# A sixteen-slot ring of expert weights in place of twelve, three of its slots filled during the output projection

## The reference

```python
mixed = concat([o_a, o_b, o_c]) @ w_out                      # (640, 2048) @ (2048, 2048)
x = x + g1 * rms_norm(mixed, g_post_mix)
h = rms_norm(x, g_pre_ffn) * (1 + sc2) + sh2
aff = softmax(h @ w_router)                                  # 16 experts
g, idx = top_k(aff.T, cap)                                   # 64 sample rows, 16 prompt rows each
hid = silu(xs @ w_gate) * (xs @ w_up)                        # per expert 2048 x 1024, twice
y = (hid @ w_down) * g                                       # per expert 1024 x 2048
x = x + g2 * rms_norm(scatter_add(y), g_post_ffn)
```

## Time and profile before

| | us |
|---|---|
| median of three runs | 2994.15 |
| lowest and highest | 2991.12, 3000.06 |
| span of the profiled execution | 2995.6 |
| PE busy in it | 2680.6 (89%) |
| DVE busy | 1331.9 (44%) |
| ACT, POOL busy | 525.4, 482.1 |
| output projection on PE, about | 1567 to 1877 |
| experts on PE, about | 1877 to 2950 |

### The profile page before, as it was taken

How to read it: one execution, slowest core, us unless ns; L and a number is a source line. 1 busy time by engine, 2 the same in 40 slices (tenths; PEclk the granted TensorE clock), 3 DMA queues, 4 the chain that set the end, 5 groups by cost and what they waited for, 6 DMA issues and landing times. The chain is left out here.

```text
span 2995.6 us, 60885 instructions
## 1 busy us (share of the span) xinstructions
PE 2680.6 (89%) x25988; PEld 1534.8 (51%) x25988; DVE 1331.9 (44%) x2353; ACT 525.4 (18%) x1471; POOL 482.1 (16%) x647
## 2 busy tenths in 40 slices
PE   5699999999959599999769999999999999999993
PEld 1366666666637489899634444333333332333330
DVE  1667667767546465666241114422233332222323
ACT  2100000000025355555331111100000000000001
POOL 0100000000065466665140000000000000000000
PEclk8899999999979799999879999999999999999996
DMA  9576555454366312221197888799999999999997
GB/s 409 210 227 208 189 180 197 174 207 173 138 204 129 131 45 53 61 52 40 26 366 267 307 308 324 309 402 404 404 405 404 404 394 396 404 404 403 403 413 290
DMA packets 268517, 783.60 MB, mean 262 GB/s; under 512 B 99473, under 2 KB 163112, under 8 KB 199712
## 3 DMA queue, kind: packets, MB, share of 16 engines
q1 hardware_dynamic: 257104, 724.13, 64.0%
q0 software_dynamic: 10848, 56.51, 6.4%
q10 hardware_dynamic: 368, 0.10, 0.0%
HBM read 712.59 MB, written 68.08 MB: 261 GB/s over the span
## 5 line engine op out<-in xcount | busy, mean ns | idle before, releaser
L2243 PE MATMUL oe_ps<-experts_ring,tail_arena 128*32 128x512 f32 x4096 | 502.8, 605 | 42.6 <-DMA experts_ring<-in_w_up 42.6
L478 DVE SCALAR_TENSOR_TENSOR pj_macc<-pj_mring,head_cond_t,pj_macc 128x1024 f32<-128x1024 f32 x240 | 297.1, 1279 | 182.1 <-DMA pj_mring<-in_w_ada 182.1
L2243 PEld LDWEIGHTS oe_ps<-experts_ring,tail_arena 128*32 128x32 f32 x4096 | 154.5, 111 | 338.8 <-issue 337.8
L551 PE MATMUL pj_ps<-head_hT,head_ring_in 128*128 128x320 f32 x1104 | 312.3, 436 | 6.5 <-DVE head_hT L451 4.2
L2276 PE MATMUL oe_ps<-experts_ring,oe_hidt 128*32 128x512 f32 x2880 | 312.1, 592 | 0.0
L2251 PE MATMUL oe_ps<-experts_ring,tail_arena 128*32 128x512 f32 x2048 | 274.3, 600 | 0.0
L551 PEld LDWEIGHTS pj_ps<-head_hT,head_ring_in 128*128 128x128 f32 x1104 | 210.9, 191 | 96.6 <-DVE head_hT L451 6.5
L2580 DVE SCALAR_TENSOR_TENSOR oe_hid_s<-oe_hid_s,oe_gcol_s,oe_ps 128x512 f32<-128x512 f32 x16 | 12.0, 748 | 535.6 <-ACT oe_hid_s L2426 535.6
L2322 PE MATMUL oe_ps<-experts_ring,tail_arena 128*128 128x512 f32 x520 | 232.5, 604 | 15.5 <-DMA tail_arena<-scratch_o 15.5
L551 PE MATMUL pj_ps<-pj_t,pj_s 128*128 128x320 f32 x736 | 210.4, 440 | 6.8 <-DVE pj_t L457 6.8
L2276 PEld LDWEIGHTS oe_ps<-experts_ring,oe_hidt 128*32 128x32 f32 x2880 | 110.2, 110 | 198.8 <-issue 198.8
(11 more groups left out here) (423 smaller groups left out, 3893.0 us busy)
## 6 DMA issues: line engine op xcount, KB each, us to landing
experts_ring<-in_w_gate SPq DMA_DIRECT2D x128, 1024.0 KB, 24.6
experts_ring<-in_w_up SPq DMA_DIRECT2D x128, 1024.0 KB, 26.2
experts_ring<-in_w_down SPq DMA_DIRECT2D x128, 1024.0 KB, 21.7
experts_ring<-in_w_out SPq DMA_DIRECT2D x68, 1024.0 KB, 6.9
pj_mring<-in_w_ada SPq DMA_DIRECT2D x64, 1024.0 KB, 9.5
head_ring_in<-in_w_in SPq DMA_DIRECT2D x23, 2048.0 KB, 7.9
ada_ring<-in_w_ada SPq DMA_DIRECT2D x16, 2048.0 KB, 19.8
scratch_z<-pj_stage POOLq DMA_DIRECT2D x19, 640.0 KB, 8.1
```

The lines of the kernel that those rows point to most:

```text
L478: a = nc.vector.scalar_tensor_tensor(acc, w, scalar, acc, ALU.mult, ALU.add)
L551: mm = pe.matmul(bank(name, b)[:, 0:TH], a[:, k, :], h[:, k, :], start=(k == 0), stop=(k == KH - 1))
L2243: pe.matmul(ps[32 * i:32 * i + 32, bank, :], xe[:, k, GROUPS[i % 2]], w[:, kk * DE + 512 * (i // 2):kk * DE + 512 * (i // 2) + 512], start ...
```

## The change

The ring gets sixteen slots: the twelve places of `experts_ring` and places 0, 1, 2 and 9 of the arena. Slab `n` goes to slot `n % 16`. Slabs 0 to 2, whose places (9 to 11) are not used by the projection, are loaded behind three chosen slabs of `w_out` in its third and fourth tile; slabs 12 to 15 are loaded when the last tile's `h2` and routing are done. Since 24 slabs an expert are not a multiple of sixteen, the loops of SP and PE now take two experts a pass. `EARLY` is half of the number of slots, so it goes from 6 to 8. What `block_final` reads changes places: `x1` and the gains go to ring slots 0 to 6, each when its slab of the last down but one is used.

```diff
+MORE = (0, 1, 2, 9)
+NSLOT = len(SLOTS) + len(MORE)
+
+FINAL_X, FINAL_G, FINAL_F = (0, 1, 2, 3, 4), (5, 6), (7, 8, 9, 10, 11)
+FINAL_FG, FINAL_JUNK = (0, 1, 2, 9, 5), 7
...
+def slot_of(ring, arena, n):
+
+    i = n % NSLOT
+    return ring[:, SLOTS[i], :] if i < len(SLOTS) else arena[:, MORE[i - len(SLOTS)], :]
...
-    SLOTS_IN = len(slot_in)
+    SLOTS_IN = NSLOT
+    FREE_AT = [(2, 3), (2, 9), (3, 3)]
...
+                if (t, j) in FREE_AT:
+                    load(0, FREE_AT.index((t, j)), FREE_AT.index((t, j)))
-            for n in range(SLOTS_IN):
-                if n >= 6:
+            for n in range(len(FREE_AT), GU):
+                if n >= len(SLOTS):
+                    if n == len(SLOTS):
+                        sp.wait_ge(h2r, NT)
+                        sp.wait_ge(routed, NT)
+                elif n >= 6:
                     sp.wait_ge(w_used, NT * SLABS - 11 + n)
-                elif n >= 3:
+                else:
                     sp.wait_ge(w_used, LAST * SLABS + 1)
-                load_expert(sp, weights, w_all, slot_in, 0, n, n)
-            for n in range(SLOTS_IN, GU):
-                load_expert(sp, weights, w_all, slot_in, 0, n, n, used=(slot_used, n - SLOTS_IN + 1))
-            with sp.Fori(1, NE) as e:
+                load(0, n, n)
+
+            def expert_loads(e, n, it):
+
                 for i in range(GU):
...
+                    load(e, i, n + i, used=(slot_used, n + i - SLOTS_IN + 1 + it * PER))
...
+            with sp.Fori(1, NE - 1, 2) as e:
+                expert_loads(e, GU, e - 1)
+                expert_loads(e + 1, GU + PER, e - 1)
+            expert_loads(NE - 1, GU + (NE - 2) * PER, 0)
...
             for t in range(NT):
-                sp.dma_start(arena[:, FINAL_X[t], :], x1_d[t]).then_inc(x1_in[t], 16)
+                sp.wait_ge(slot_used, base - DN + FINAL_X[t] + 1)
+                sp.dma_start(w_all[:, SLOTS[FINAL_X[t]], :], x1_d[t]).then_inc(x1_in[t], 16)
...
-            with pe.Fori(2, NE - 1) as e:
-                expert(e)
+            expert(1, GU, None)
+            with pe.Fori(2, NE - 2, 2) as e:
+                expert(e, GU + PER, e - 2)
+                expert(e + 1, GU + 2 * PER, e - 2)
+            expert(NE - 2, GU + (NE - 3) * PER, None)
```

More of the change, by code:

```diff
@@ L1991, in _, with load_expert @@
                 finish_pair(q)
-def load_expert(sp, weights, ring, slot_in, e, r, n, used=None):
+def slot_of(ring, arena, n):
+    i = n % NSLOT
+    return ring[:, SLOTS[i], :] if i < len(SLOTS) else arena[:, MORE[i - len(SLOTS)], :]
+def load_expert(sp, weights, ring, arena, slot_in, e, r, n, used=None):
     w_gate, w_up, w_down = weights
-    slot = n % len(slot_in)
-    place = SLOTS[slot]
+    slot, place = n % NSLOT, slot_of(ring, arena, n)
     e = bass.ds(e, 1)
@@ L2003, in load_expert @@
         src = w[0, e, (r // 2) * 256:(r // 2 + 1) * 256, :].rearrange("o (p k) f -> p (o k) f", p=P)
-        dst = ring[:, place, :].rearrange("p (k f) -> p k f", k=2)
+        dst = place.rearrange("p (k f) -> p k f", k=2)
     else:
         src = w_down[0, e, (r - 16) * P:(r - 15) * P, :].rearrange("o p f -> p (o f)")
-        dst = ring[:, place, :]
+        dst = place
     if used:
@@ L2116, in _, with load @@
                 sp.dma_start(crow[(2 + cnd) * KD:(3 + cnd) * KD, :], mod_d[cnd, 3 * D:4 * D].rearrange("(k p) -> k p", p=P)).then_inc(once, 16)
+            def load(e, r, n, used=None):
+                load_expert(sp, weights, w_all, arena, slot_in, e, r, n, used)
             for n in range(RING, NT * SLABS):
@@ L2136, in _ @@
                 for i in range(DN):
-                    load_expert(sp, weights, w_all, slot_in, e - 1, GU + i, 2 * GU + i, used=(slot_used, (e - 1) * PER + 2 * GU + i - SLOTS_IN + 1))
+                    load(e - 1, GU + i, n + i, used=(slot_used, n + i - SLOTS_IN + 1 + it * PER))
+            with sp.Fori(1, NE - 1, 2) as e:
+                expert_loads(e, GU, e - 1)
+                expert_loads(e + 1, GU + PER, e - 1)
+            expert_loads(NE - 1, GU + (NE - 2) * PER, 0)
             base = GU + (NE - 1) * PER
@@ L2139, in _ @@
             for i in range(DN):
-                load_expert(sp, weights, w_all, slot_in, NE - 1, GU + i, base + i, used=(slot_used, base + i - SLOTS_IN + 1))
+                load(NE - 1, GU + i, base + i, used=(slot_used, base + i - SLOTS_IN + 1))
             for t in range(NT):
-                sp.dma_start(arena[:, FINAL_X[t], :], x1_d[t]).then_inc(x1_in[t], 16)
+                sp.wait_ge(slot_used, base - DN + FINAL_X[t] + 1)
+                sp.dma_start(w_all[:, SLOTS[FINAL_X[t]], :], x1_d[t]).then_inc(x1_in[t], 16)
@@ L2143, in _ @@
             for cnd in range(2):
-                sp.dma_start(arena[:, FINAL_G[cnd], :], bcast_rows(cst_d, (3 * cnd + 2) * D, D)).then_inc(g2_in, 16)
+                sp.wait_ge(slot_used, base - DN + FINAL_G[cnd] + 1)
+                sp.dma_start(w_all[:, SLOTS[FINAL_G[cnd]], :], bcast_rows(cst_d, (3 * cnd + 2) * D, D)).then_inc(g2_in, 16)
         @block.gpsimd
@@ L2235, in slabs_of @@
             def slabs_of(j, n0):
-                return w_all[:, SLOTS[(n0 + 2 * j) % SLOTS_IN]], w_all[:, SLOTS[(n0 + 2 * j + 1) % SLOTS_IN]]
+                return slot_of(w_all, arena, n0 + 2 * j), slot_of(w_all, arena, n0 + 2 * j + 1)
             def sample_step(xe, j, kk, n0):
@@ L2630, in sem @@
             return nc.alloc_semaphore("fi_" + name)
-        f, junk, fg = ring[:, 0:NT], ring[:, NT], ring[:, NT + 1:2 * NT + 1]
-        x, g2 = [arena[:, i, :] for i in FINAL_X], [arena[:, i, :] for i in FINAL_G]
+        f, x, g2 = ([ring[:, SLOTS[i], :] for i in at] for at in (FINAL_F, FINAL_X, FINAL_G))
+        fg, junk = [arena[:, i, :] for i in FINAL_FG], arena[:, FINAL_JUNK, :]
         st, eps = sb("st", [P, NT, 3]), sb("eps", [P, 1])
```

24 lines of the change are left out of this document (11 added, 13 removed).

## The result

The changed kernel takes 3004.36 us in the median (3002.49 to 3010.92) beside 2994.87 of the kernel before on the same chip (2991.12 to 3000.65): ratio 1.0032, 95% interval 1.0021 to 1.0042, 9.5 us slower by the medians. Forecast was 2990.7 us, between 2983 and 2999. The profiled execution has a span of 3002.4 us.

A forecast was written before the change was run, and what follows sets the result against it. The prediction took the full DMA queue of expert weights as the bound. From a span of 2995.6 us, -4.1 for the stream and +0.6 for instructions gave 2992.1, a median of 2990.7 us, range 2983 to 2999.

The forecast's parts named there:

- What bounds the kernel: From the restart of the weight stream to the last down, the DMA queue is full at 421 GB/s; PE has slack.
- Four more slots: At the restart of the weight stream, sixteen slabs are there instead of twelve: 9.96 us of the stream done.
- `EARLY`: Four more sample steps ahead of the first prompt step let the first pair go 6.88 us later.
- the gather: Expert 1's gather falls into the DMA hole instead of the restart: adds 0 to 2.54 us, taken as 1.0.
- Three early slabs: Three slabs loaded in the projection move 7.5 us of loading; cost nothing, gain 0 to 0.7 us, taken as 0.
- the wait on SP: SP's new wait on `h2r` and `routed` has only slabs 12 to 15 and slabs waiting for `slot_used` behind it.
- the end: Loads of `x1` and the gains, now waiting for the last down but one, stay hidden: no cost, otherwise 2.5 us.
- Loops of two experts: Two more experts written out cost 0.6 us of instruction packets; PE's larger loop body isn't fetched again, so costs nothing.
- Rival 1: PE's loop is fetched again each pass, as traffic only: 3.0 us more, 2993.7 us in all; chance 0.20.
- Rival 2: PE stands still at the head of each pass, five times, and becomes the bound: 3026.7 or 3010 us; chance 0.08.
- Rival 3: In expert 0, PE waits 1.9 us for prompt rows gathered among four slabs: 2992.5 us; chance 0.14.
- Rival 4: All seven slabs loaded ahead count at the restart, 10.5 us gained: 2983.6 us; chance 0.10.

## Why the prediction was wrong

**What bounds the kernel: right.** The stream of weights sets the end. Whatever delayed or advanced it moved the end, and taking PE's "issue" stalls away hardly did.

**Four more slots, `EARLY`, the gather: right.** Slab 16 at 1916.34 for 1916.62, expert 1 begun 2.3 us ahead of 1933.10, and the stream 4.4 us ahead for a forecast of 4.1 (4.0 without the earlier routing). The version that has only these terms gained 5.4 us by its profile.

**Three early slabs, the wait on SP, the end: right.** Without the early fills the time is the same. The last matmuls leave as much of the span behind them as before:

```profile
2952.81 3.61 PE L2302 MATMUL oe_ps<-tail_arena,oe_hidt_last 128*32 128x512 f32 x32
```

That is 3002.4 - (2952.81 + 3.61) = 46.0 us; before it was 2995.6 - (2932.78 + 16.84) = 46.0.

**"Loops of two experts": the step that failed**, twice. "By the row it costs nothing" took one expert's body, which stays, for two experts'. The body of 2304 is fetched again on every pass: 64 packets more on the page (55 were worked out for that case). And the price was wrong: "0.065 us each" divides a packet's time by sixteen engines. A slab counts when its last part has landed, and a packet of PE's, which delays eight parts of sixteen, costs 0.18 us. 64 x 0.18 = 11.5 us, the loss of the run with the loop alone; -4.1 + 11.5 = 7.4, and 9.5 by the medians and 6.8 by the spans were measured. The prediction had seen that a single engine's price would be more and left it to the rivals, where none had it.

The rule cited from the Trainium skill (Runtime: NRT & Kernel Launch, "Instruction fetch mechanics") gives PE room for 2048 instructions. These traces agree with it: a loop of about 1152 stayed, one of about 2304 didn't. The prediction called the row a disagreement, but one expert's loop fits that room, so the row and this figure never stood against each other, and the figure was the better guide to the larger loop. The stall that this section of the Trainium skill warns of did come, 3.9 us a pass, but the kernel without it was still 6.2 us slower than the one before. The same section of the Trainium skill prefers code written out; here that had nearly the same packets (207 beside 216) and was about as slow.

**The rivals.** Rival 1 (traffic only) had the mechanism, with 0.6 + 3.0 = 3.6 us for the 11.5. Rival 2 had PE's stall at the right place and its bound held: up to 5.0 to 6.7 us a pass it is free, and 3.9 us were nearly free. Rival 3 did not come: the prompt rows were turned at 1906.77 + 2.85 = 1909.62, and PE wanted them at 1914.23:

```profile
1906.77 2.85 DVE L2519 STREAM_TRANSPOSE tail_arena<-tail_arena 32x512 f32<-32x512 f32 x4 [7.38 <-DMA tail_arena<-scratch_h,oe_tok_p]
1914.23 10.48 PE L2277 MATMUL oe_ps<-experts_ring,tail_arena 128*32 128x512 f32 x96
```

It did come, at 1.97 us, where the prompt steps weren't moved. Rival 4 fell with the run without early fills.

## What to carry to other kernels

When the DMA engines are full, code that has to be fetched is traffic on the critical path: count the instruction packets a change adds, and price them by how late they make the last part of a load, not by the mean of sixteen engines. Keep the body of a loop small enough that it isn't fetched again, even where the engine that runs it has slack. And a ring needn't be deeper for good to start better: a few slabs loaded once into idle places give the same start without a change to the loops.

## What the runs showed of the hardware

- PE's loop of about 1152 instructions had no packet in four passes; one of about 2304 was fetched again on each of five returns, 64 packets more with the code written out beside it, and PE stood still for 3.7 to 4.0 us at its head.
- PE's instruction packets delayed eight of a slab's sixteen parts, in all five kernels that had more of them, and cost the stream 0.18 us for each of 16 KB. GpSimd's packets (queue 14, 8 KB) delayed one part of sixteen, by 0.65 us each; the times give 0.50 and 0.72 us each.
- None of that shows in the DMA share: from 1930 to 2960 the queues of the changed kernel add up to 100.3% of the sixteen engines' time, those of the kernel before to 100.6%. It shows in how far apart a slab's parts land.
